# The identity in the chunks' state matrices: sixteen TensorE products per group, or an addend of VectorE

## The chip, the cores and the metric

One NeuronCore of a Trainium2 chip runs the program. The metric is device microseconds (us) of one execution. Engines run their own instruction streams in order and meet only through semaphores: TensorE (PE), VectorE (DVE), ScalarE (ACT), GpSimd (POOL) and SyncE (SP, which here issues the DMAs). TensorE writes to PSUM, and VectorE and ScalarE read it from there.

## The reference, cut to what matters

Two blocks on 512 tokens of width 1024 in f32. The second has a time mixing with one recurrence per token and head (8 heads of 64):

```
state = state * w_t + sa[..., None] * (kk_t * a_t) + v_t[..., None] * k_t
y_t   = einsum('bhvk,bhk->bhv', state, r_t)          # sa = state @ (-kk_t)
```

The kernel does this in chunks of 64 tokens. Over a chunk the state goes through a matrix of the form "decay times (identity plus a product)" and gets an addend. The identity of that sum is what this case is about.

## The kernel before, in words

The second block covers the last 280 us or so of the program. Its input projection and output projection are products of 128x128 weights with 128x512 activations, each as three f32r products (lines 621 to 623: high with high, high with low, low with high). A tile of weights is split by ScalarE (L1293, `whi`) and VectorE (L1845, `wlo`).

The heads are taken in four groups f = 0 to 3 of two heads (128 channels). For each group there are two generators on every engine: `prep(f)` (token shift, decay, keys; beside the projection tiles of window f) and `rwkv(f)` (the chunk algebra; beside the tiles of window f + 1, for f = 3 beside the output projection). `step()` takes one piece of `rwkv` and then one piece of `prep`. It runs on TensorE after every three projection products, and on the other engines at the same count, so the `yield`s of each engine say at which projection step a piece is queued. All order is written out by hand in this way, and no engine overtakes itself.

In `rwkv(f)` the part around the change runs as follows.

- VectorE (L2471) and ScalarE (L1737) copy the solved matrices `QG` out of PSUM.
- TensorE forms, for 8 chunks of 2 heads, the 16 transposed 64x64 matrices `QG` with `Bn` (L1134) and adds to each the identity, as a product of `I64` with itself (L1137), in banks 3 and 4. `s_p` then counts 3f + 1. Then come the chunks' addends (L1142, L1145) in banks 5 and 6, and `s_p` counts 3f + 2. Two heads and two chunk parities take the four 64x64 quarters of the array in turn.
- ScalarE copies the 16 matrices into `Pb` (L1744, two instructions of 64 partitions, one for each head) and counts `s_pv`. `Pb` is block diagonal, and its zeros were written once by GpSimd.
- VectorE scales the addends into `CS` (L2476) and counts `s_pe`.
- The chain over chunks c = 1 to 6: TensorE multiplies `Pb` of c by the state `CS` of c (L1158), VectorE scales and adds (L2486) and gives the next state. The first L1158 waits for `s_pv` and `s_pe`, the others for the L2486 before them. Between them TensorE does the products of L1162, L1168 and L1173 and three projection products for each step.

VectorE runs `prep(f + 1)` in between: L2364 to L2385 (keys), L2314 and L2316 (token shift), L2392 and L2395.

Of the kernel before, what the change touches and what calls it, by code (L numbers as in the profile page):

```python
# [9 lines left out]
ALU = mybir.AluOpType  # L10
ACTF = mybir.ActivationFunctionType
# [22 lines left out]
def build_program(nc, A, out, blocks):  # L34
# [91 lines left out]
    Z = {n[0]: t for n, t in zip(names2, region(0, *names2))}  # L126
# [8 lines left out]
    BK = [PS[:, i, :] for i in range(8)]  # L135
# [133 lines left out]
    s_q, s_qa, s_qd, s_p, s_pv, s_pe = (sem(n) for n in ("s_q", "s_q_act", "s_q_dve", "s_p", "s_p_act", "s_p_dve"))  # L269
# [18 lines left out]
    for q in range(32):  # L288
        g, j = divmod(q, 4)
# [97 lines left out]
    pair = lambda b: PS[:, b:b + 2, 0:256].rearrange("p a (b t) -> p a b t", b=4)  # L387
# [207 lines left out]
    def pe_program(pe):  # L595
# [83 lines left out]
        for c in range(NC):  # L679
            ms = pe.matmul(BK[7][:, c * 128:(c + 1) * 128], small[:, 4 + c:5 + c].to_broadcast([P, P]), ident[:, :],  # L680
                           start=True, stop=True)
# [171 lines left out]
        for j in range(8):  # L853
            half, jj = divmod(j, 4)
            t = tile0[("v", j)]
# [3 lines left out]
            for c in range(NC):  # L859
# [4 lines left out]
                for kk in range(2):  # L864
# [3 lines left out]
                    ms = pe.matmul(h4(bank[:, :]), Hh[:, k, tok], wlo[s][:, at, :], start=False, stop=k == KT - 1)  # L868
# [161 lines left out]
        HALF = [slice(0, 64), slice(64, 128)]  # L1030
        QUADS = [(par, h) for par in range(2) for h in range(2)]

        def rwkv(f):
            KR, bt, kt = Z[f"KR{f % 2}"], Z[f"bt{f % 2}"], Z[f"kt{f % 2}"]
            Vn, Bn, Kn, KA, QG = (Z[n] for n in ("Vn", "Bn", "Kn", "KA", "QG"))
            Ln, Xx, Tt, AU, RB, RK, Ww = (Z[n] for n in ("Ln", "Xx", "Tt", "AU", "RB", "RK", "Ww"))
            Pb, Sb, CS, Rp, I64, YT = (Z[n] for n in ("Pb", "Sb", "CS", "Rp", "id64", "YT"))
            nat = lambda t, par, h, j: t[HALF[par], j * 128 + h * 64:j * 128 + h * 64 + 64]
# [24 lines left out]
            for j in range(4):  # L1063
                for par, h in QUADS:
                    c = 2 * j + par
                    ms = pe.matmul(BK[5 + h][HALF[par], j * 64:(j + 1) * 64], KR[HALF[h], 0, c * 64:(c + 1) * 64],
                                   bt[HALF[h], c * 64:(c + 1) * 64], start=True, stop=True)
# [12 lines left out]
            for j in range(4):  # L1080
                for par in range(2):
                    for h in range(2):
                        ms = pe.matmul(BK[5 + par][HALF[par], j * 128 + h * 64:j * 128 + h * 64 + 64],
                                       mat(AU, par, h, j), nat(Vn, par, h, j), start=True, stop=True)
# [4 lines left out]
            for q in range(1, 6):  # L1089
# [4 lines left out]
                for j in range(4):  # L1094
                    for par, h in QUADS:
                        ms = pe.matmul(BK[3 + par][HALF[h], j * 64:(j + 1) * 64], mat(Ln, par, h, j), mat(Xx, par, h, j),  # L1096
                                       start=True, stop=True)
# [4 lines left out]
                for j in range(4):  # L1102
                    for par, h in QUADS:
                        ms = pe.matmul(BK[5 + par][HALF[h], j * 64:(j + 1) * 64], mat(Xx, par, h, j), I64[HALF[par], :],  # L1104
                                       start=True, stop=True)
# [4 lines left out]
                for j in range(4):  # L1110
                    for par, h in QUADS:
                        ms = pe.matmul(BK[3 + h][HALF[par], j * 64:(j + 1) * 64], matT(Tt, par, h, j), matT(Ww, par, h, j),  # L1112
                                       start=True, stop=True)
# [7 lines left out]
            for j in range(4):  # L1121
                for par, h in QUADS:
                    ms = pe.matmul(BK[3 + 2 * par + h][HALF[par], j * 128:(j + 1) * 128], mat(Xx, par, h, j),
                                   KA[HALF[par], j, h, :, :], start=True, stop=True)
# [6 lines left out]
            pe.wait_ge(s_nat, 4 * f + 4)  # L1131
            for j in range(4):
                for par, h in QUADS:
                    pe.matmul(BK[3 + par][HALF[h], j * 64:(j + 1) * 64], QG[HALF[par], h, j, 0, :], nat(Bn, par, h, j),  # L1134
                              start=True, stop=False)
                for par, h in QUADS:
                    ms = pe.matmul(BK[3 + par][HALF[h], j * 64:(j + 1) * 64], I64[HALF[par], :], I64[HALF[par], :],  # L1137
                                   start=False, stop=True)
            ms.then_inc(s_p, 1)
            for j in range(4):  # L1140
                for par, h in QUADS:
                    pe.matmul(BK[5 + par][HALF[h], j * 64:(j + 1) * 64], nat(Kn, par, h, j), nat(Vn, par, h, j),  # L1142
                              start=True, stop=False)
                for par, h in QUADS:
                    ms = pe.matmul(BK[5 + par][HALF[h], j * 64:(j + 1) * 64], nat(Bn, par, h, j), QG[HALF[par], h, j, 1, :],  # L1145
                                   start=False, stop=True)
# [5 lines left out]
            for c in range(1, 7):  # L1152
# [6 lines left out]
                if c == 1:  # L1159
                    for j in range(4):  # L1160
                        for par, h in QUADS:
                            ms = pe.matmul(BK[3 + par][HALF[h], j * 64:(j + 1) * 64], QG[HALF[par], h, j, 0, :],  # L1162
                                           mat(RB, par, h, j), start=True, stop=True)
                    ms.then_inc(s_p, 1)
                if c == 2:
                    for j in range(4):
                        for par, h in QUADS:
                            pe.matmul(BK[5 + par][HALF[h], j * 64:(j + 1) * 64], nat(Vn, par, h, j), mat(RK, par, h, j),  # L1168
                                      start=j == 0, stop=False, skip_group_check=True)
# [9 lines left out]
            for c in range(1, 8):  # L1179
                j, par = divmod(c, 2)  # L1180
# [42 lines left out]
        t = tile0[("o7", 6)]  # L1223
# [9 lines left out]
        t = tile0[("o8", 0)]  # L1233
# [39 lines left out]
    def act_program(act):  # L1273
# [430 lines left out]
        def rwkv(f):  # L1704
            KA, QG, Pb, Sb, CS = (Z[n] for n in ("KA", "QG", "Pb", "Sb", "CS"))
            for i in range(REST if f == 0 else 0):
                yield
            act.wait_ge(s_q, f)
            act.activation(c8(Z["Xx"][:, :]), Z["id64"][:, :].unsqueeze(1).to_broadcast([P, 8, 64]),
                           ACTF.Copy).then_inc(s_id, 1)  # L1710
            natural(f, 0, Z["Vn"][:, :])
            for i in range(3):
                yield
            for i in range(2):
                yield
            act.wait_ge(s_gr, 4 * f + 4)
            act.activation(KA[0:64, :, :, 1, :], BK[5][0:64, :].rearrange("p (j h v) -> p j h v", j=4, h=2),
                           ACTF.Copy).then_inc(s_avc, 1)
            act.wait_ge(s_nt, 4 * f + 2)
            act.activation(KA[:, :, :, 0, :], BK[7][:, :].rearrange("p (j h k) -> p j h k", j=4, h=2),  # L1720
                           ACTF.Copy).then_inc(s_nat, 1)
            yield
            for q in range(1, 6):
                n = 5 * f + q
                act.wait_ge(s_lw, 2 * n - 1)
                act.activation(Z["Ww"][:, :].rearrange("p (a t) -> p a t", a=2), PS[:, 3:5, 0:256],
                               ACTF.Copy).then_inc(s_ww, 1)
                act.wait_ge(s_lw, 2 * n)
                act.activation(Z["Tt"][:, :].rearrange("p (a t) -> p a t", a=2), PS[:, 5:7, 0:256],
                               ACTF.Copy).then_inc(s_ww, 1)  # L1730
                yield
                yield
                if q <= 2:
                    natural(f, 1 + q, Z[("Bn", "Kn")[q - 1]][:, :])
                yield
            act.wait_ge(s_q, f + 1)
            act.activation(QG[0:64, :, :, :, :].rearrange("p h j a t -> p h (j a t)"), PS[0:64, 3:5, :],  # L1737
                           ACTF.Copy).then_inc(s_qa, 1)
            yield
            yield  # L1740
            act.wait_ge(s_p, 3 * f + 1)
            for h in range(2):
                hs = slice(64 * h, 64 * h + 64)
                e = act.activation(Pb[hs, :, hs].rearrange("p (j a) t -> p a j t", a=2), pair(3)[hs, :, :, :], ACTF.Copy)  # L1744
            e.then_inc(s_pv, 1)
            yield
            yield
            if f in (1, 2):
                yield
            for c in range(1, 7):  # L1750
                if c == 4:
                    act.wait_ge(s_sc, 6 * f + 3)
                    for h in range(2):
                        hs = slice(64 * h, 64 * h + 64)
                        e = act.activation(Sb[hs, 1:5, hs], CS[hs, 1:5, :], ACTF.Copy)
                    e.then_inc(s_sb, 1)
                yield
            act.wait_ge(s_sc, 6 * f + 6)
            for h in range(2):
                hs = slice(64 * h, 64 * h + 64)  # L1760
                e = act.activation(Sb[hs, 5:8, hs], CS[hs, 5:8, :], ACTF.Copy)
            e.then_inc(s_sb, 1)
            yield
            act.wait_ge(s_y, f + 1)
            act.wait_ge(s_gn, f)
            if f == 0:
                act.wait_ge(s_x2, 9)
            act.activation(Z["YT"][:, :].rearrange("p (j a t) -> p a j t", j=4, a=2), pair(5), ACTF.Copy).then_inc(s_yc, 1)
            yield
            act.wait_ge(s_gmd, f + 1)  # L1770
            act.activation(Z["GQ"][:, :], Z["YT"][:, :], ACTF.Square).then_inc(s_gs, 1)
            yield
            yield
            for i in range((4, 7, 0, 0)[f]):
                yield
            act.wait_ge(s_gm, 2 * f + 2)
            act.activation(Z["GQ"][:, :], BK[7][:, :], ACTF.Sqrt, bias=GEPS, scale=1.0 / 64).then_inc(s_gs, 1)
            yield
            yield
# [39 lines left out]
    def dve_program(v):  # L1819
# [312 lines left out]
        for c in range(NC):  # L2132
            e = v.tensor_scalar(V[:, c, :], V[:, c, :], small[:, 16 + c:17 + c], None, ALU.mult)
# [297 lines left out]
        def rwkv(f):  # L2431
# [39 lines left out]
            v.tensor_copy(QG[64:128, :, :, :, :].rearrange("p h j a t -> p h (j a t)"), PS[64:128, 5:7, :]).then_inc(s_qd, 1)  # L2471
            yield
            yield
            v.wait_ge(s_p, 3 * f + 2)
            v.wait_ge(s_ip, f + 1)
            v.tensor_tensor(CS[:, 1:9, :].rearrange("p (j a) t -> p a j t", a=2), pair(5),  # L2476
# [178 lines left out]
```

## Time and profile before

| | |
|---|---|
| median of 3 runs | 1449.18 us (1447.69 to 1449.83) |
| the profiled execution, its own time | 1447.83 us |
| its span, first to last instruction | 1446.6 us |
| mean granted TensorE clock | 0.996 of 2.4 GHz |
| busy: TensorE, VectorE, ScalarE | 99%, 61%, 43% of the span |

The time outside the span is 1447.83 − 1446.6 = 1.2 us. Busy shares are averages over the whole program. What a change in one stage is worth is read from the order in which the engines reach their waits there, so most of the rows below are instructions in order of time. f32 products of lines 1134 to 1173 are seen in the trace as two passes each, so the 64 identity products of the program are 128 rows.

### The profile page before, as it was taken

Reading aid. Unit: us, or ns where it says so; the run is one execution under the profiler, and the core shown is the slowest. Engines: PE = TensorE matmul, PEld = TensorE weight load, DVE = VectorE, ACT = ScalarE, POOL = GpSimd, SP = SyncE. Lnnn points to the kernel's source line nnn. Section 1 sums busy time; section 2 is a strip of 40 time slices with the busy share of each in tenths; the row PEclk is TensorE's granted clock in tenths of the full one; section 3 lists DMA queues with packets and bytes.
Section 4 is the critical chain, followed back from the end, with each engine's and each line's share of the span. In section 5 each row is a group of like instructions: output and inputs, shape, how many; then the busy total and the mean of one; then the engine's idle time right before and its main releaser. Section 6 shows DMA issues by size and latency. Waiting matters only on the chain.

```text
span 1446.6 us, 25206 instructions
## 1 busy us (share of the span) xinstructions
PE 1426.7 (99%) x9965; PEld 1141.6 (79%) x9965; DVE 882.3 (61%) x1251; ACT 625.6 (43%) x976; POOL 195.9 (14%) x228
## 2 busy tenths in 40 slices
PE   8999999999999999999999999999999999999898
PEld 5788888887888887888878888888888777777677
DVE  4777777777545756855556432344345876666736
ACT  4665655555554323232334322244233454453535
POOL 0000000000048888800006000000000000000000
PEclk9999999999999999999999999999999999999999
DMA  9454443444355665533323333333332311211111
GB/s 336 122 148 117 135 114 110 138 125 123 104 157 167 174 173 156 168 98 88 102 73 103 98 101 93 91 98 102 102 88 73 88 47 46 59 45 43 44 51 59
DMA packets 266188, 157.69 MB, mean 109 GB/s; under 512 B 5797, under 2 KB 254938, under 8 KB 266074
## 3 DMA queue, kind: packets, MB, share of 16 engines
q1 hardware_dynamic: 266074, 156.07, 37.0%
q8 instruction: 83, 1.36, 0.4%
q14 instruction: 31, 0.25, 0.1%
HBM read 153.82 MB, written 2.23 MB: 108 GB/s over the span
## 4 chain that ended last, share of the span: by engine, by line
PE 92%; DVE 4%; ACT 2%; issue 1%; POOL 0%; DVEq 0%; ACTq 0%; POOLq 0%
PE PS L621 24%; PE PS L622 23%; PE PS L623 23%; PE PS L796 1%; PE PS L866 1%; PE PS L822 1%; PE PS L868 1%; PE PS L867 1%; PE PS L1096 1%; PE PS L1112 1%; DVE Hl L1857 1%; PE PS L654 1%; PE PS L801 1%; PE PS L813 1%; PE PS L1104 1%
## 5 line engine op out<-in xcount | busy, mean ns | idle before, releaser
L621 PE MATMUL PS<-Hh,whi 128*128 128x512 f32 x1162 | 477.5, 411 | 2.8 <-DVE Hl L1857 2.3
L623 PE MATMUL PS<-Hh,wlo 128*128 128x512 f32 x1162 | 453.6, 390 | 0.0
L622 PE MATMUL PS<-Hl,whi 128*128 128x512 f32 x1162 | 453.5, 390 | 0.0
L1845 DVE TENSOR_TENSOR wlo<-raw,whi 128x1024 fp32r<-128x1024 f32 (+1 forms) x211 | 280.5, 1330 | 111.8 <-ACT whi L1293 111.0
L1293 ACT ACTIVATE whi<-raw 128x1024 fp32r<-128x1024 f32 (+1 forms) x211 | 221.2, 1048 | 167.9 <-PE PS L623 145.6
L621 PEld LDWEIGHTS PS<-Hh,whi 128*128 128x128 f32 x1162 | 218.3, 188 | 64.7 <-issue 18.6
L623 PEld LDWEIGHTS PS<-Hh,wlo 128*128 128x128 f32 x1162 | 218.2, 188 | 46.6
L622 PEld LDWEIGHTS PS<-Hl,whi 128*128 128x128 f32 x1162 | 218.6, 188 | 44.9 <-issue 4.8
L519 POOL TENSOR_TENSOR mbuf<-mbuf,cact 128x1024 f32<-128x1024 f32 x32 | 63.0, 1968 | 414.8 <-DMA mbuf<-in_w_mod_dram 414.8
L621 PE MATMUL PS<-YBh,whi 128*128 128x512 f32 x256 | 99.6, 389 | 0.0
L622 PE MATMUL PS<-YBl,whi 128*128 128x512 f32 x256 | 99.6, 389 | 0.0
L623 PE MATMUL PS<-YBh,wlo 128*128 128x512 f32 x256 | 99.6, 389 | 0.0
L524 POOL TENSOR_TENSOR mbuf<-mbuf 128x512 f32<-128x512 f32 x64 | 90.6, 1416 | 5.0
L1986 DVE SCALAR_TENSOR_TENSOR tmp<-xr,pcA,tmp 128x512 f32<-128x512 f32 x96 | 71.7, 747 | 6.9 <-ACT tmp L1381 5.4
L2267 DVE TENSOR_TENSOR tmp<-tmp 128x512 f32<-128x512 f32 x32 | 22.2, 693 | 56.1 <-ACT tmp L1581 56.1
L623 PEld LDWEIGHTS PS<-YBh,wlo 128*128 128x128 f32 x256 | 48.0, 188 | 10.1
L621 PEld LDWEIGHTS PS<-YBh,whi 128*128 128x128 f32 x256 | 48.0, 188 | 10.0
L622 PEld LDWEIGHTS PS<-YBl,whi 128*128 128x128 f32 x256 | 48.0, 188 | 9.9
L1581 ACT ACTIVATE tmp<-PS 128x512 f32<-128x512 f32 x32 | 19.1, 597 | 74.9 <-PE PS L623 73.5
L621 PE MATMUL PS<-R2h,whi 128*128 128x512 f32 x128 | 50.2, 392 | 0.0
L622 PE MATMUL PS<-R2l,whi 128*128 128x512 f32 x128 | 49.8, 389 | 0.0
L623 PE MATMUL PS<-R2h,wlo 128*128 128x512 f32 x128 | 49.8, 389 | 0.0
(411 smaller groups left out, 1879.4 us busy)
## 6 DMA issues: line engine op xcount, KB each, us to landing
raw<-in_w_in_dram SPq DMA_DIRECT2D x106, 512.0 KB, 3.9
raw<-in_w_ff_dram SPq DMA_DIRECT2D x64, 512.0 KB, 3.6
mbuf<-in_w_mod_dram SPq DMA_DIRECT2D x32, 512.0 KB, 3.7
wm<-in_w_mod_dram SPq DMA_DIRECT2D x8, 1024.0 KB, 9.6
crow<-cum_rows SPq DMA_DIRECT2D x32, 256.0 KB, 4.5
raw<-in_w_branch_ssm_dram SPq DMA_DIRECT2D x16, 512.0 KB, 3.4
erow<-exp_rows SPq DMA_DIRECT2D x24, 256.0 KB, 5.0
raw<-in_w_out_dram SPq DMA_DIRECT2D x10, 512.0 KB, 3.4
```

What stands on the lines that cost most here:

```text
L519: pool.tensor_tensor(w[:, :, :], w[:, :, :], cact[:, :].unsqueeze(2).to_broadcast([P, KT, P]), ALU.mult).then_inc(s_pool, 1)
L524: pool.tensor_tensor(w[:, 0:n, :], w[:, 0:n, :], w[:, n:2 * n, :], ALU.add).then_inc(s_pool, 1)
L621: pe.matmul(bank[:, :], whi[s][:, k, :], xh[:, kk, :], start=kk == 0, stop=False)
L622: pe.matmul(bank[:, :], whi[s][:, k, :], xl[:, kk, :], start=False, stop=False)
L623: last = pe.matmul(bank[:, :], wlo[s][:, k, :], xh[:, kk, :], start=False, stop=t == end - 1 and k == (order or range(kt))[-1])
L654: pe.matmul(h4(BK[bank][:, :]), identb[:, :], identb[:, :].unsqueeze(1).to_broadcast([P, 4, P]), start=True, stop=True)
L796: ms = pe.matmul(to(a), xdt[n % 2][:, h * 64:(h + 1) * 64], dec[n % 2][:, h * 128:(h + 1) * 128], start=True, stop=c == 0)
L1293: act.activation(whi[s][:, 0:kt, :], raw[s][:, 0:kt, :], ACTF.Copy).then_inc(s_whi, 1)
L1581: act.activation(q[:, :], bank[:, :], ACTF.Relu).then_inc(s_relu, 1)
L1845: v.tensor_tensor(wlo[s][:, 0:kt, :], raw[s][:, 0:kt, :], whi[s][:, 0:kt, :].bitcast(F32), ALU.subtract).then_inc(s_wlo, 1)
L1986: e = v.scalar_tensor_tensor(out=a[:, :], in0=b[:, tap:tap + T], scalar=cw(tap, tile), in1=a[:, :], op0=ALU.mult, op1=ALU.add)
L2267: v.tensor_tensor(q[:, :], q[:, :], q[:, :], ALU.mult).then_inc(s_f2, 1)
```

## The change: what it does, and the diff

TensorE no longer multiplies the identity with itself. VectorE takes over the two copies into `Pb` from ScalarE and adds the identity on the way, `id64` being read again for each of the 8 matrices of an instruction. It does so in `rwkv`, after the copy of `QG` and ahead of the scaling into `CS`. The semaphores stay as they were: the adds wait for `s_p` at 3f + 1 and count `s_pv`.

```diff
@@ pe rwkv
             for j in range(4):
                 for par, h in QUADS:
-                    pe.matmul(BK[3 + par][HALF[h], j * 64:(j + 1) * 64], QG[HALF[par], h, j, 0, :], nat(Bn, par, h, j),
-                              start=True, stop=False)
-                for par, h in QUADS:
-                    ms = pe.matmul(BK[3 + par][HALF[h], j * 64:(j + 1) * 64], I64[HALF[par], :], I64[HALF[par], :],
-                                   start=False, stop=True)
+                    ms = pe.matmul(BK[3 + par][HALF[h], j * 64:(j + 1) * 64], QG[HALF[par], h, j, 0, :],
+                                   nat(Bn, par, h, j), start=True, stop=True)
             ms.then_inc(s_p, 1)
@@ act rwkv
             yield
             yield
-            act.wait_ge(s_p, 3 * f + 1)
-            for h in range(2):
-                hs = slice(64 * h, 64 * h + 64)
-                e = act.activation(Pb[hs, :, hs].rearrange("p (j a) t -> p a j t", a=2), pair(3)[hs, :, :, :], ACTF.Copy)
-            e.then_inc(s_pv, 1)
             yield
             yield
@@ dve rwkv
             yield
             yield
+            v.wait_ge(s_p, 3 * f + 1)
+            for h in range(2):
+                hs = slice(64 * h, 64 * h + 64)
+                e = v.tensor_tensor(Z["Pb"][hs, :, hs].rearrange("p (j a) t -> p a j t", a=2), pair(3)[hs, :, :, :],
+                                    Z["id64"][hs, :].unsqueeze(1).unsqueeze(1).to_broadcast([64, 2, 4, 64]), ALU.add)
+            e.then_inc(s_pv, 1)
             v.wait_ge(s_p, 3 * f + 2)
```

VectorE in group 0, kernel before: from the last weight split (`wlo`) to the chain's second step; `wk`, `kt`, `tmp`, `rb` belong to `prep(1)`.

```order
L1845 TENSOR_TENSOR wlo2<-raw2,whi2 128x1024 [waits s_tile,s_whi]
L2382 TENSOR_TENSOR wk4<-wk4,tmp1 128x512 [waits s_dve_own]
L2476 TENSOR_TENSOR CS<-PS,fx0 128x2x4x64 [waits s_fx,s_p]
L2385 TENSOR_TENSOR kt1<-wk4,wk3 128x512 [waits s_dve_own]
L2314 TENSOR_TENSOR tmp0<-pad1 128x512 [waits s_shift,s_pad]
L2316 SCALAR_TENSOR_TENSOR rb<-tmp0,pcC,pad1 128x512 [waits s_dve_own]
L2486 SCALAR_TENSOR_TENSOR CS<-PS,fx0,CS 128x64 [waits s_p_dve,s_s] x2
```

The same place in the changed kernel (its lines from L1134 on have lower numbers: L2474 is L2476 of before, L2484 is L2486).

```order
L1837 TENSOR_TENSOR wlo2<-raw2,whi2 128x1024 [waits s_tile,s_whi]
L2374 TENSOR_TENSOR wk4<-wk4,tmp1 128x512 [waits s_dve_own]
L2469 TENSOR_TENSOR Pb<-PS,id64 64x2x4x64 [waits s_p]
L2469 TENSOR_TENSOR Pb<-PS,id64 64x2x4x64
L2474 TENSOR_TENSOR CS<-PS,fx0 128x2x4x64 [waits s_fx,s_p]
L2377 TENSOR_TENSOR kt1<-wk4,wk3 128x512 [waits s_dve_own]
L2306 TENSOR_TENSOR tmp0<-pad1 128x512 [waits s_shift,s_pad]
L2308 SCALAR_TENSOR_TENSOR rb<-tmp0,pcC,pad1 128x512 [waits s_dve_own]
L2484 SCALAR_TENSOR_TENSOR CS<-PS,fx0,CS 128x64 [waits s_p_dve,s_s] x2
```

Two instructions stand between the keys' product and the scaling into `CS`. Everything behind them on VectorE keeps its order, and the first step of the chain over chunks is the fourth instruction behind the scaling.

VectorE in groups 1 and 2, changed kernel (shown of group 1); before, the rows are the same without the two of L2469.

```order
L2463 COPY QG<-PS 64x1024 [waits s_q]
L2356 SCALAR_TENSOR_TENSOR KR0<-acc,wk0 128x512 [waits s_decay_exp]
L2361 SCALAR_TENSOR_TENSOR acc<-wk1,acc 128x512 [waits s_dve_own,s_sigm]
L2469 TENSOR_TENSOR Pb<-PS,id64 64x2x4x64 [waits s_p]
L2469 TENSOR_TENSOR Pb<-PS,id64 64x2x4x64
L2474 TENSOR_TENSOR CS<-PS,fx1 128x2x4x64 [waits s_fx,s_p]
L2365 TENSOR_TENSOR acc<-acc,tmp1 128x512 [waits s_dve_own]
```

Here the two adds come directly behind L2361, the L2369 of before, and ahead of the same scaling.

## Rows read from the trace of the kernel before

**Rows 1.** The page: busy time of the engines with share of the span

```profile
PE 1426.7 (99%) x9965; PEld 1141.6 (79%) x9965; DVE 882.3 (61%) x1251; ACT 625.6 (43%) x976; POOL 195.9 (14%) x228
```

**Rows 2.** The page: chain that ended last, by engine

```profile
PE 92%; DVE 4%; ACT 2%; issue 1%; POOL 0%; DVEq 0%; ACTq 0%; POOLq 0%
```

**Rows 3.** Groups by shape, 1180 to 1410 us: count | busy us, mean ns | idle, releaser

```profile
L1744 ACT ACTIVATE Pb<-PS 64x512 f32<-64x512 f32 x8 | 4.7, 591 | 5.9 <-PE PS L1137 5.8
...
L1137 PE MATMUL PS<-id 64*64 64x64 f32 x128 | 4.0, 218 | 0.0
...
L2476 DVE TENSOR_TENSOR CS<-PS,fx 128x512 f32<-128x512 f32 x4 | 2.8, 692 | 3.5 <-PE PS L1145 3.5
```

**Rows 4.** Waits, 1180 to 1410 us: us in total, times, longest

```profile
DVE CS L2476 <- PE PS L1145: 3.5, 3, 1.7
...
PEld PS L1158 <- DVE CS L2486: 1.4, 3, 0.5
...
PE PS L1005 <- DVE acc L2556: 2.8, 1, 2.8
```

**Rows 5.** Timeline, group 0, TensorE: start us, us, engine, line [idle before <-releaser]

```profile
1191.50 0.30 PE L1137 MATMUL PS<-id 64*64 64x64 f32 x8
...
1192.32 0.30 PE L1142 MATMUL PS<-Vn,Kn 64*64 64x64 f32 x8
...
1194.63 0.41 PEld L1158 LDWEIGHTS PS<-CS,Pb 128*128 128x128 f32 x2
...
1196.63 0.30 PEld L1158 LDWEIGHTS PS<-CS,Pb 128*128 128x128 f32 x2 [0.37 <-DVE CS L2486]
```

**Rows 6.** Timeline, group 0, VectorE

```profile
1192.99 0.68 DVE L2382 TENSOR_TENSOR wk<-wk,tmp 128x512 f32<-128x512 f32 x1
1193.71 0.69 DVE L2476 TENSOR_TENSOR CS<-PS,fx 128x512 f32<-128x512 f32 x1
1194.32 0.68 DVE L2385 TENSOR_TENSOR kt<-wk 128x512 f32<-128x512 f32 x1
...
1196.30 0.28 DVE L2486 SCALAR_TENSOR_TENSOR CS<-PS,fx,CS 128x64 f32<-128x64 f32 x1
1197.11 0.28 DVE L2486 SCALAR_TENSOR_TENSOR CS<-PS,fx,CS 128x64 f32<-128x64 f32 x1 [0.53 <-PE PS L1158]
```

**Rows 7.** Timeline, group 1, all engines

```profile
1256.30 0.69 DVE L2369 SCALAR_TENSOR_TENSOR acc<-wk,acc 128x512 f32<-128x512 f32 x1
...
1257.87 0.69 DVE L2476 TENSOR_TENSOR CS<-PS,fx 128x512 f32<-128x512 f32 x1 [0.88 <-PE PS L1145]
...
1259.92 0.55 DVE L2379 TENSOR_SCALAR tmp<-wk,kah,omka 128x512 f32<-128x512 f32 x1
...
1260.38 1.22 DVE L1845 TENSOR_TENSOR wlo<-raw,whi 128x1024 fp32r<-128x1024 f32 x1
...
1261.52 0.28 DVE L2486 SCALAR_TENSOR_TENSOR CS<-PS,fx,CS 128x64 f32<-128x64 f32 x1
...
1261.85 0.30 PEld L1158 LDWEIGHTS PS<-CS,Pb 128*128 128x128 f32 x2 [0.53 <-DVE CS L2486]
```

**Rows 8.** Timeline, group 3, all engines

```profile
1398.15 0.30 PE L1137 MATMUL PS<-id 64*64 64x64 f32 x8
...
1398.51 1.19 ACT L1744 ACTIVATE Pb<-PS 64x512 f32<-64x512 f32 x2 [1.69 <-PE PS L1137]
...
1399.44 0.69 DVE L2476 TENSOR_TENSOR CS<-PS,fx 128x512 f32<-128x512 f32 x1 [1.69 <-PE PS L1145]
...
1400.80 0.33 PE L1158 MATMUL PS<-CS,Pb 128*128 128x64 f32 x2
```

**Rows 9.** Windows: us, busy of each engine, then PEclk, DMA share, GB/s

```profile
360.00:362.00 2.00, 0.50 (x3) 0.40 (x3) 0.69 (x1) 1.87 (x4) 0.00 (x0) 1.00 0.95 292
362.00:364.00 2.00, 2.00 (x12) 1.61 (x11) 0.00 (x0) 0.25 (x1) 0.00 (x0) 1.00 0.85 188
...
1364.00:1365.00 1.00, 1.00 (x10) 0.35 (x12) 1.00 (x3) 0.00 (x0) 0.00 (x0) 0.50 0.00 0
```

## The prediction, made before the changed kernel was run

> **What bounds the kernel now.** I read the page first, then the grouped instructions and the waits of the stretch in which the changed lines run, and last the timeline around each of the four groups. TensorE is busy 99% of the span and VectorE 61% [rows 1], and the chain that ended last lies to 92% on TensorE [rows 2]. By these averages alone, work taken from TensorE is time won, and VectorE has room. The waits say that this does not hold at the place of the change. TensorE stood three times at the chain over chunks, at a L1158 that waited for VectorE's L2486, 1.4 us in all [rows 4]. In group 0 this was the second L1158, at 1196.63 us after 0.37 us of idleness [rows 5]. In group 1 it was again the second, at 1261.85 us after 0.53 us [rows 7]. The third, in group 2, is the same pattern. So in groups 0 to 2 VectorE sets the time of this point, and only in group 3 does TensorE. The reason is VectorE's queue: it runs without idle time from L2382 at 1192.99 us to L2486 at 1196.30 us, since the chain's first step is queued behind three instructions of the next group's preparation [rows 6].
>
> **What goes from TensorE.** The 64 products with the identity are 128 passes [rows 3]. Their mean of 218 ns is not their price, because four quarters of the array overlap. The price is the step between starts: from the run of L1137 at 1191.50 us to the run of L1142 at 1192.32 us there are seven runs of 8 passes (L1137 and L1134 in turn) [rows 5], so 8 passes take 0.82 / 7 = 0.117 us, 14.6 ns each. A group has 32 such passes, 0.47 us, and the four groups 1.87 us. That is the most the change could give.
>
> The Trainium skill has a floor for this: "TensorE: Matmul & The Clock Gate", section "Back-to-back issue gap", lets no matmul of up to 64 columns start less than about 25 ns behind another. By it a group's passes would be worth 0.80 us instead of 0.47, and the sum below would be 0.33 us lower, since only group 3 keeps this gain. The trace speaks against it, with 14.6 ns for passes in different quarters.
>
> **What goes from ScalarE.** Eight copies of 0.591 us [rows 3] go. ScalarE had been idle 1.69 us before them in group 3 [rows 8], and what stood behind them are copies and weight splits whose takers on VectorE are queued behind other VectorE work: in group 1 the next `wlo` starts only at 1260.38 us, directly behind L2379 [rows 7]. Worth nothing, and the cover is VectorE's own queue. Were that cover gone, nothing would be lost either, because this edit only frees.
>
> **What comes to VectorE.** Two adds per group, each of 64 partitions and 512 elements, PSUM and `id64` in, `Pb` out. The trace has no such instruction. The nearest is L2476: two operands, one of them broadcast, the other from the same kind of PSUM pair, 512 elements, 0.692 us long [rows 3]. But the next instruction starts 0.61 us after it (1193.71 to 1194.32 us) [rows 6], so what it costs the queue is p = 0.61 us. Upper bound: the step from L2382 to L2476, 0.72 us. Lower bound: the step from L2379 to L1845, 0.46 us (1259.92 to 1260.38) [rows 7], an instruction with one tensor operand. I take 0.61.
>
> A page speaks against moving such a copy: "Advanced Engine Details and Errata", section "The Read-Write Bubble", of the Trainium skill says that VectorE exposes the memories' latency between two instructions, and that ScalarE lies nearer to PSUM. The trace agrees in part: 0.692 us on VectorE against 0.591 us on ScalarE, while successive instructions overlap by 0.08 us. With the whole 0.69 us for p the sum would be +1.8 us.
>
> **Group 0.** The queue has no gap, so the adds push L2476, L2385, L2314, L2316 and the first L2486 by 2p = 1.22 us. The first L1158 waits for L2476, which ended at 1194.40 and would end at 1195.62 us. TensorE would come there at 1194.63 − 0.47 = 1194.16 us and stand for some 1.4 us. The second L1158 waits for the first L2486, 1196.30 + 1.22 = 1197.52 us instead of 1196.30, so it starts 1.22 us later than 1196.63. The second L2486 then waits for TensorE again, as before (0.53 us [rows 6]), and from there on both engines carry the same delay. TensorE's 0.47 us lies inside this wait and is lost. Group 0: +1.22 us.
>
> **Groups 1 and 2.** Here VectorE had been idle 0.88 us before L2476 (of the 3.5 us in three waits [rows 4]: 0.88, 0.88, 1.69). L1134 is through 0.47 us sooner, so `s_p` is there when L2369 leaves the queue free, at 1256.30 + 0.61 = 1256.91 us. L2476 then starts at 1256.91 + 1.22 = 1258.13 instead of 1257.87 us: +0.26 us. From there to L2486 at 1261.52 us there is no gap [rows 7], so the second L1158 comes 0.26 us later, and TensorE's 0.47 us again only lengthens its wait. In general 2p − 0.96 for each. Groups 1 and 2: +0.52 us.
>
> **Group 3.** The output projection gives VectorE little to do. The last L1137 began at 1398.15 us and ScalarE took up its result at 1398.51 us, 0.36 us later [rows 8]. In the changed kernel the result is there 0.47 us sooner, at 1398.04 us; the adds take 1.22 us, and L2476 runs from 1399.26 to 1399.95 us (its own operand is there at 1399.44 − 0.47 = 1398.97 us). TensorE reaches the first L1158 at 1400.80 − 0.47 = 1400.33 us, with its weight load some 0.2 us ahead of that. The wait is met with 0.2 us to spare, and the 0.47 us is won: −0.47 us. It is lost from 2p of about 1.4 us on.
>
> **Sum.** 1.22 + 0.52 − 0.47 = +1.27 us, in general 6p − 2.39 us: +0.4 us for p = 0.46 and +1.9 us for p = 0.72. Nothing later gives the delay back, since the waits behind these points are for results that follow from them. This is against the profiled execution's 1447.83 us (span 1446.6 and 1.2 around it), which gives 1449.1 us. That execution lies 1.35 us under the median of the runs, 1449.18 us, and the changed kernel is measured by a median too, so I forecast 1449.18 + 1.27, rounded 1450.5 us.
>
> **Rivals.**
>
> 1. TensorE's saving is the time: −1.87 us, 1447.3 us. For it speak the 99% and the 92% [rows 1, 2]. It needs VectorE's delay to be absorbed, and VectorE had no idle time between L2382 and L2486 [rows 6]. Partly true (some of group 0's delay absorbed later) it gives about 1449 us, no change.
> 2. The adds are dear, and the kernel is slower by more than 0.2%. The place is VectorE's queue ahead of L2476, in all four groups. If the broadcast and the strided `Pb` doubled the work, p would be near the 1.14 us step of a 1024 element instruction (L1845 at 1260.38 to L2486 at 1261.52 [rows 7]): 6 × 1.14 − 2.39 = +4.45 us, and group 3 pays another 2.28 − 1.4 = 0.9 us, together 1454.5 us. It decides from p = 0.88 us on (+2.9 us). Against it: L2476 has the same shape and a broadcast, and ScalarE's copy into the same strides took 0.591 us.
> 3. The clock. TensorE's new stand of about 1.4 us in group 0 could take it to the lower level. After its longest stand in this stretch, 2.8 us ahead of L1005 [rows 4], the granted clock was 0.50 at 1364 us, the 1.2 GHz level, while after 1.5 us idle within 360 to 362 us it stayed at 1.00, 2.4 GHz [rows 9]. If it fell for 4 us (I assume this length), work of 2 us would take 4: +2 us on top, 1452.5 us. The nearer row says that it holds.
>
> **How the numbers follow.** About 0.2%, 2.9 us, is what a measurement of this kernel can tell from no change. The forecast (its own range 1449.5 to 1451.5 us) has a chance of 0.66, rival 1 in full or in part 0.16, rival 2 0.10, rival 3 0.08. The forecast lies within 0.2% altogether, and so does nearly all of rival 1; half of rival 3 and all of rival 2 do not. With medians that differ by some tenths from one measurement to the next this makes faster 0.04, same 0.81, slower 0.15. The range of 8 in 10 takes the bounds of p, +0.4 and +1.9 us, and the runs' own spread of 2.1 us: 1448.4 to 1452.5 us.
>
> **What would show it.** Right: the adds at 0.6 to 0.7 us each, back to back; a wait of TensorE of over 1 us at the first L1158 of group 0 with L2476's counterpart as its releaser; the wait at the second L1158 of groups 1 and 2 grown from 0.53 to about 1.3 us; no new wait in group 3, and there the distance from the first L1134 to the first L1158 shorter by 0.47 us. Wrong: an add over 0.85 us; no growth of TensorE's waits in groups 0 to 2 although the products are gone; a granted clock under 1.00 between 1195 and 1202 us.

## The result, and the profile after

| | median us | runs | range |
|---|---|---|---|
| before | 1449.13 | 20 | 1447.10 to 1451.36 |
| after | 1452.12 | 20 | 1448.88 to 1455.76 |

The ratio is 1.0019, with a 95% interval of 1.0012 to 1.0026: slower by 1.7 to 3.8 us. The ratio lies just inside the 0.2% that the prediction had called no change, the upper end of its interval outside. Later the changed kernel was measured again, under the label e10_again: 1450.78 us against 1448.98, ratio 1.0012 (1.0003 to 1.0021). A small loss is sure. Its size is easier to read from the trace.

The profiled execution of after took 1453.63 us, 5.80 more than that of before. Most of this has nothing to do with the change. The first L1134 of group 0, ahead of which no changed instruction runs, already began 3.66 us later (1191.33 and 1194.99 us), because the clock was low twice more on the way there than before. The windows show it: time, busy of each engine, granted clock, DMA share, GB/s. First after, then before.

```profile
14.00:18.00 4.00, 3.88 (x24) 1.98 (x28) 3.63 (x7) 0.00 (x0) 0.00 (x0) 0.62 1.11 370
574.00:578.00 4.00, 3.25 (x9) 2.26 (x8) 4.00 (x6) 0.63 (x1) 1.51 (x2) 0.59 0.00 0
```

```profile
14.00:18.00 4.00, 4.00 (x42) 1.61 (x40) 2.31 (x4) 0.38 (x1) 0.00 (x0) 1.00 1.11 371
574.00:578.00 4.00, 4.00 (x19) 3.33 (x20) 4.00 (x8) 2.21 (x3) 1.59 (x2) 1.00 0.19 56
```

So I compare distances in which this cancels as long as the clock within them is alike: from the first weight load of L1134 in a group to that in the next, and from the last to the end of the span. The timelines of before at groups 0, 1 and 3, then of after:

```profile
1191.33 0.21 PEld L1134 LDWEIGHTS PS<-Bn,QG 64*64 64x64 f32 x8 [0.37 <-issue]
...
1255.71 0.21 PEld L1134 LDWEIGHTS PS<-Bn,QG 64*64 64x64 f32 x8 [0.36 <-issue]
...
1397.28 0.21 PEld L1134 LDWEIGHTS PS<-Bn,QG 64*64 64x64 f32 x8 [0.36 <-issue]
```

```profile
1194.99 0.56 PEld L1134 LDWEIGHTS PS<-Bn,QG 64*64 64x64 f32 x32 [0.37 <-issue]
...
1260.81 0.56 PEld L1134 LDWEIGHTS PS<-Bn,QG 64*64 64x64 f32 x32 [0.37 <-issue]
...
1403.55 0.56 PEld L1134 LDWEIGHTS PS<-Bn,QG 64*64 64x64 f32 x32 [0.36 <-issue]
```

Group 0 takes 65.82 us instead of 64.38 (+1.44), group 1 67.63 instead of 67.03 (+0.60), group 2 75.11 instead of 74.54 (+0.57; it begins at 1322.74 us before and at 1328.44 after). From there the end comes after 48.75 instead of 49.32 us (−0.57). That last stretch holds much work behind the chain, so for group 3 I also use the distance to the load of `GQ`'s product (L1191, after: L1188): 16.95 and 16.56 us, −0.39. The whole is +2.04 us by the span. In the second execution of after (e10_again) the four are +1.42, +0.61, +0.58 and −0.40, by the span +1.86. Inside group 2 the clock was low once in before (at 1364 us) and once in after (at 1370 us), and not at all in e10_again; the distance of e10_again is nevertheless after's to 0.01 us.

The page after, engines' busy time, in answer to [rows 1]:

```profile
PE 1428.6 (98%) x9837; PEld 1141.8 (79%) x9837; DVE 889.0 (61%) x1259; ACT 621.2 (43%) x968; POOL 195.6 (13%) x228
```

128 matmul rows (64 products of two passes) and 8 copies fewer, 8 adds more, and the shares hardly move. What moved are the waits, 1180 to 1412 us, in answer to [rows 4] (us in total, times, longest):

```profile
PE PS L1155 <- DVE CS L2484: 2.4, 3, 1.1
...
PEld PS L1155 <- DVE CS L2484: 3.7, 3, 1.6
PE PS L1155 <- DVE CS L2474: 1.4, 1, 1.4
```

L1155 is the chain's product (L1158 before), L2474 and L2484 are VectorE's L2476 and L2486. The three waits of the weight loads grew from 1.4 to 3.7 us, and one more of 1.4 us came at the start of group 0's chain. Group 0 after, VectorE and TensorE, in answer to [rows 5, 6]:

```profile
1196.65 0.69 DVE L2374 TENSOR_TENSOR wk<-wk,tmp 128x512 f32<-128x512 f32 x1
1197.37 1.39 DVE L2469 TENSOR_TENSOR Pb<-PS,id 64x512 f32<-64x512 f32 x2
1198.79 0.69 DVE L2474 TENSOR_TENSOR CS<-PS,fx 128x512 f32<-128x512 f32 x1
1199.40 0.68 DVE L2377 TENSOR_TENSOR kt<-wk 128x512 f32<-128x512 f32 x1
...
1199.63 0.41 PE L1155 MATMUL PS<-CS,Pb 128*128 128x64 f32 x2 [1.42 <-DVE CS L2474]
...
1201.72 0.30 PEld L1155 LDWEIGHTS PS<-CS,Pb 128*128 128x128 f32 x2 [0.60 <-DVE CS L2484]
```

The two adds hold the queue from 1197.37 to 1198.79 us, 0.71 us each, and TensorE stands 1.42 us at the chain's first product. Group 1, in answer to [rows 7]:

```profile
1261.39 0.69 DVE L2361 SCALAR_TENSOR_TENSOR acc<-wk,acc 128x512 f32<-128x512 f32 x1
1262.11 1.39 DVE L2469 TENSOR_TENSOR Pb<-PS,id 64x512 f32<-64x512 f32 x2
1263.54 0.69 DVE L2474 TENSOR_TENSOR CS<-PS,fx 128x512 f32<-128x512 f32 x1
...
1267.52 0.30 PEld L1155 LDWEIGHTS PS<-CS,Pb 128*128 128x128 f32 x2 [1.55 <-DVE CS L2484]
```

VectorE now has no gap here, and the wait at the second L1155 grew from 0.53 to 1.55 us. Group 3, in answer to [rows 8]:

```profile
1404.32 1.39 DVE L2469 TENSOR_TENSOR Pb<-PS,id 64x512 f32<-64x512 f32 x2 [0.29 <-PE PS L1134]
1405.74 0.69 DVE L2474 TENSOR_TENSOR CS<-PS,fx 128x512 f32<-128x512 f32 x1
1406.55 0.30 PEld L1155 LDWEIGHTS PS<-CS,Pb 128*128 128x128 f32 x2 [0.21 <-issue]
```

TensorE comes with almost no wait: this is the one group in which its time was won. From the first L1134 to the first chain product it takes 3.05 us (1403.56 to 1406.61), 0.47 us less than before, as in e1 below; the 0.21 us of idle time ahead of the weight load is new, and some 0.05 us of the gain is gone at the next load. The clock behind group 0's new stand stayed at its upper level, 1.00 (2.4 GHz), in answer to [rows 9]:

```profile
1201.00:1203.00 2.00, 1.84 (x38) 1.27 (x37) 1.47 (x5) 0.00 (x0) 0.00 (x0) 1.00 0.00 0
```

### The profile page after: what moved, and what is told of

The parts are those of the page before. It is cut to its first block, busy times and chain, and to the rows that moved or that the text cites. A ratio compares the mean times of both kernels' runs of the same rounds, so it can differ in the third digit from the quotient of the medians.

```text
span 1452.3 us, 24950 instructions
## 1 busy us (share of the span) xinstructions
PE 1428.6 (98%) x9837; PEld 1141.8 (79%) x9837; DVE 889.0 (61%) x1259; ACT 621.2 (43%) x968; POOL 195.6 (13%) x228
## 4 chain that ended last, share of the span: by engine, by line
PE 92%; DVE 5%; ACT 2%; issue 1%; POOL 0%; DVEq 0%; POOLq 0%; ACTq 0%
PE PS L621 24%; PE PS L622 23%; PE PS L623 23%; PE PS L796 1%; PE PS L866 1%; PE PS L822 1%; PE PS L867 1%; PE PS L868 1%; PE PS L1096 1%; PE PS L654 1%; PE PS L1112 1%; DVE Hl L1849 1%; PE PS L801 1%; PE PS L813 1%; PE PS L1104 1%
```

## The experiments

Each was read by the distances above. The table gives them as differences from before (g3 is the distance to `GQ`'s product). The ratio is that of the times, with its 95% interval.

| | g0 | g1 | g2 | g3 | ratio |
|---|---|---|---|---|---|
| after | +1.44 | +0.60 | +0.57 | −0.39 | 1.0019 (1.0012 to 1.0026) |
| e10_again | +1.42 | +0.61 | +0.58 | −0.40 | 1.0012 (1.0003 to 1.0021) |
| e1_products_gone | −0.03 | −0.46 | −0.48 | −0.46 | 0.9984 (0.9975 to 0.9993) |
| e2_add_beside | +1.38 | +0.61 | +0.56 | +0.05 | 1.0013 (1.0004 to 1.0022) |
| e3b_full_identity | +1.42 | +0.61 | +0.59 | −0.40 | one time, 1452.28 us |
| e4b_adds_twice | +4.29 | +4.89 | +4.83 | +0.98 | 1.0080 (1.0062 to 1.0097) |
| e5_split | −0.01 | −0.01 | +0.02 | −0.38 | 0.9997 (0.9988 to 1.0006) |
| e6_one_step_later | +0.74 | +0.58 | +0.58 | −0.40 | 1.0014 (1.0003 to 1.0024) |
| e7_split_later | −0.23 | 0.00 | +0.01 | −0.38 | 0.9996 (0.9987 to 1.0006) |
| e8_one_add | +0.95 | +0.11 | +0.21 | +0.07 | 1.0004 (0.9995 to 1.0012) |
| e9_compact | +0.40 | +0.37 | +0.43 | +0.55 | 1.0007 (0.9998 to 1.0016) |

**The halves of the change.** e1 is the kernel before with TensorE's edit alone:

```diff
-                for par, h in QUADS:
-                    ms = pe.matmul(BK[3 + par][HALF[h], j * 64:(j + 1) * 64], I64[HALF[par], :], I64[HALF[par], :], ...)
```

> Only TensorE's part of the change: the 16 identity products of a group are gone, ScalarE still copies Pb, VectorE adds nothing, so the identity is left out of the chunks' matrices. Measure: the distance from a group's first L1134 to the next group's (for group 3 to the end of the span), 64.38, 67.03, 74.54 and 49.3 us before. Theory A (VectorE's queue sets the time in groups 0 to 2, TensorE in group 3): group 0 unchanged (0.0), because the first L2486 stands behind VectorE's own queue; groups 1 and 2 shorter by 0.47 us each, because there VectorE had been idle before L2476 and starts it 0.47 us sooner; group 3 shorter by 0.47; together -1.4 us. Theory B (TensorE's saving counts everywhere and the loss comes from elsewhere, as from the clock): -0.47 us in each group, -1.9 us.

The removal saves 0.46 to 0.48 us in three groups and nothing in group 0, where the weight load of TensorE's second chain product stood 0.60 us instead of 0.37:

```profile
1195.92 0.30 PEld L1155 LDWEIGHTS PS<-CS,Pb 128*128 128x128 f32 x2 [0.60 <-DVE CS L2483]
```

In groups 1 and 2 the saving is real without the adds, since VectorE's 0.88 us of idleness there [rows 7] shrinks with it. There it was TensorE that VectorE waited for.

e2 is the changed kernel with the identity's products put back (the diff of e1 reversed); the identity is then counted twice.

> Only VectorE's and ScalarE's part: the identity products stay on TensorE, and VectorE's two adds replace ScalarE's copies, so the identity is counted twice. Theory A: group 0 +1.43 us (two adds of 0.71 us in a queue without a gap), groups 1 and 2 +0.58 each (the adds start when L2369 leaves the queue free, whether the products are there or not), group 3 about +0.1 (the adds end a little after TensorE arrives), together +2.7 us. Theory B: no change, 0 us.

With the products there, groups 0 to 2 are as slow as without them, and only group 3 changes, by 0.44 us. So the two halves don't add up: in the changed kernel TensorE's saving is worth 0.4 us, where e1 has 1.43. The rest is shut into VectorE's waits.

**Why an add costs 0.71 us and not 0.61.** e3b is the changed kernel; it lets the adds read an ordinary tile that holds the identity eight times, in place of the repeated operand:

```diff
+                    own(v.tensor_copy(c8(tmp[2][:, :]), Z["id64"][:, :].unsqueeze(1).to_broadcast([P, 8, 64])))
...
-                                    Z["id64"][hs, :].unsqueeze(1).unsqueeze(1).to_broadcast([64, 2, 4, 64]), ALU.add)
+                                    two(tmp[2][hs, :]), ALU.add)
```

> The changed kernel, but the adds take the identity from a tile that holds it eight times (filled once, before group 0) instead of reading one 64x64 block again for each matrix. Theory A1 (the 0.71 us instead of 0.61 us from start to start belong to instructions with a repeated operand): each add starts 0.61 us after its predecessor, L2474's counterpart still 0.72 us after the second add; the distance from a group's first L1134 to the next one's is 1.2 us longer than before in group 0 and 0.35 in groups 1 and 2. Theory A2 (they belong to the half of the partitions, the strided output, or PSUM): 0.71 us, and the distances of the changed kernel, +1.44, +0.60 and +0.57 us.

```profile
1195.54 0.68 DVE L2374 TENSOR_TENSOR wk<-wk,tmp 128x512 f32<-128x512 f32 x1
1196.26 1.39 DVE L2471 TENSOR_TENSOR Pb<-PS,tmp 64x512 f32<-64x512 f32 x2
1197.68 0.69 DVE L2476 TENSOR_TENSOR CS<-PS,fx 128x512 f32<-128x512 f32 x1
```

Still 1.42 us for two, so the repeated operand is not the reason. e8 makes the two one add of 128 partitions, with `Pb` kept without its zero blocks and a chain step of two 64x64 products:

```diff
-                pe.matmul(BK[7][:, 0:64], Pb[:, c, :], CS[:, c, :], start=True, stop=True).then_inc(s_s, 1)
+                for h in range(2):
+                    ms = pe.matmul(BK[7][HALF[h], 0:64], Pb[HALF[h], c, 0:64], CS[HALF[h], c, :], start=True, stop=True)
+                ms.then_inc(s_s, 1)
...
+            v.tensor_tensor(Z["Pb"][:, :, 0:64].rearrange("p (j a) t -> p a j t", a=2), pair(3),
```

> The changed kernel with a compact Pb (128 partitions x 8 chunks x 64, the zeros left out): one add of 128 partitions fills it, and a step of the chain over chunks is two 64x64 products in two quarters of the array in place of one 128x128. Theory A: VectorE carries one add instead of two: 0.71 us if each instruction costs that whatever its partitions (A2a), 0.61 if half partitions were what cost the 0.10 us (A2b). The first chain product then comes 0.7 us sooner than in the changed kernel in group 0, and against before group 0 +0.7 us, groups 1 and 2 -0.1 to 0, group 3 -0.4, apart from what the chain's products in quarters cost or save, which no row of before shows; that part is read from the run beside it. Theory B (the queue of VectorE is not what counts): the first chain product of group 0 as late as in the changed kernel.

```profile
1194.80 0.68 DVE L2376 TENSOR_TENSOR wk<-wk,tmp 128x512 f32<-128x512 f32 x1
1195.52 0.69 DVE L2469 TENSOR_TENSOR Pb<-PS,id 128x512 f32<-128x512 f32 x1
1196.13 0.68 DVE L2474 TENSOR_TENSOR CS<-PS,fx 128x512 f32<-128x512 f32 x1
```

The one add on all partitions is followed after 0.61 us, an add on 64 after 0.71, though both last 0.69 us. The strided output isn't the reason either: the two adds that e4b (below) puts into scratch, with no gaps between the matrices, take 1.40 us.

But half the partitions can't be the whole reason. The 128-partition add of e8 itself starts 0.72 us behind L2376 (1194.80 to 1195.52 us), without overlap, and so does L2476 in the kernel before, 0.72 us behind L2382 [rows 6]. These steps share something else with those of the 64-partition adds: the first partition changes. The copy of `QG`, VectorE's last read of PSUM ahead of them, begins at partition 64 and the instruction at 0; in the changed kernel the adds begin at 0 and at 64, and the scaling at 0 again. In e8 the add and the scaling both begin at 0, and they overlap. No run has two instructions on 64 partitions with the same first partition behind one another, so that the change of the first partition is the reason, and not the width, fits all these rows but was not tested by itself.

e8 also changes the chain, so e9 has this by itself: the kernel before with e8's chain products and one copy of ScalarE for the two.

> The kernel before with the same compact Pb: the identity products stay, ScalarE copies Pb in one instruction of 128 partitions, and the chain's steps are two 64x64 products. It shows what the chain in quarters costs or saves by itself. Theory A: no change up to the first chain product (ScalarE's copy was not waited for). From there on between -0.2 and +0.2 us per step, 24 steps: -4.8 to +4.8 us; I take 0, since a change of the array's form is made before each step now instead of behind it.

A chain in quarters is dearer, 0.37 to 0.55 us per group of six steps, 1.75 us in all, 0.07 us a step on average. The steps differ. In group 0 the third one, which other products in quarters follow, takes 1.05 us from the projection product ahead of it to the one behind (before: 1.12); the fourth, between projection products alone, takes 0.59 us (before: 0.37). Ahead of such a step TensorE has an issue gap, which in the kernel before stands nowhere ahead of the chain's last four products of this group:

```profile
1200.13 0.14 PEld L1159 LDWEIGHTS PS<-CS,Pb 64*64 64x64 f32 x2 [0.37 <-issue]
...
1201.76 0.19 PEld L1159 LDWEIGHTS PS<-CS,Pb 64*64 64x64 f32 x4 [0.36 <-issue]
```

Against e9 the single add is worth +0.55, −0.26, −0.22 and −0.48 us. The prediction's forms with one add of 0.61 give +0.61, −0.35, −0.35 and −0.47; the 0.72 us ahead of the add accounts for the 0.1 us or so that groups 1 and 2 lack.

**How the loss grows.** e4b puts two further adds, into scratch, ahead of the two:

```diff
+                v.tensor_tensor(two(tmp[2][hs, :]), pair(3)[hs, :, :, :],
+                                Z["id64"][hs, :].unsqueeze(1).unsqueeze(1).to_broadcast([64, 2, 4, 64]), ALU.add)
```

> The changed kernel with VectorE's adds doubled: ahead of the two adds into Pb stand two of the same shape into a scratch tile. Theory A (VectorE's queue sets the time): another 2 x 0.71 = 1.43 us in each of groups 0, 1 and 2, so distances from L1134 to L1134 of 67.2, 69.1 and 76.5 us, and in group 3, from the first L1134 to the load of GQ's product, 18.0 us instead of 16.56; against the kernel before +7.8 us. Theory B (the adds are hidden, the loss is elsewhere): the distances of the changed kernel, 65.8, 67.6, 75.1 and 16.6 us.

The weight load of the first chain product moved by what was expected, 1.40, 1.41 and 1.40 us in groups 0 to 2, and group 3 grew over after by 1.37 us. But groups 0 to 2 grew by 2.85, 4.29 and 4.26 us. The windows of e4b show where the rest lies:

```profile
1196.00:1198.00 2.00, 0.00 (x0) 0.00 (x0) 1.94 (x4) 0.00 (x0) 0.00 (x0) 1.00 0.70 208
1200.00:1202.00 2.00, 1.83 (x37) 1.33 (x35) 1.44 (x5) 0.00 (x0) 0.00 (x0) 0.68 0.00 0
1202.00:1204.00 2.00, 2.00 (x13) 1.59 (x16) 0.52 (x2) 0.00 (x0) 0.00 (x0) 0.50 0.03 8
1270.00:1272.00 2.00, 2.00 (x35) 1.69 (x32) 1.31 (x3) 0.00 (x0) 0.00 (x0) 0.50 0.85 235
```

```profile
1265.96 0.41 PE L1155 MATMUL PS<-CS,Pb 128*128 128x64 f32 x2 [1.08 <-DVE CS L2478]
1269.11 0.69 PE L1155 MATMUL PS<-CS,Pb 128*128 128x64 f32 x2 [1.22 <-DVE CS L2488]
```

In group 0 TensorE stood 2.83 us until 1198.36; the granted clock fell behind this and was 0.50, the 1.2 GHz level, at 1202 us. An estimate from the windows: 2 us at 0.68 and 2 us at 0.50 are 1.6 us of full speed, about the 1.45 us that group 0 grew beyond the adds. In group 1 (and in group 2 alike) the clock fell, 0.75 in the window from 1268 to 1270 us and 0.50 after it, behind two stands of 1.08 and 1.22 us, each shorter than the changed kernel's 1.42 in its group 0. So the prediction's third rival exists. The changed kernel's one stand of 1.42 us didn't set it off in either profile, but a longer one did, and so did two shorter ones that followed one another.

**Where VectorE has room.** e5 is the kernel before with the change made only where the waits allowed it: in group 3 for both halves, in groups 1 and 2 for one, in group 0 not at all.

```diff
+    ADDED = {0: (), 1: (1,), 2: (1,), 3: (0, 1)}
...
+                                   nat(Bn, par, h, j), start=True, stop=h in ADDED[f])
...
+                    if h not in ADDED[f]:
+                        ms = pe.matmul(BK[3 + par][HALF[h], j * 64:(j + 1) * 64], I64[HALF[par], :], I64[HALF[par], :],
```

> The change put only where VectorE has room: group 0 as before, groups 1 and 2 half (head 1 by VectorE's add, head 0 by 8 identity products and ScalarE's copy), group 3 wholly. Theory A: group 0 unchanged; groups 1 and 2 shorter by 0.23 us each (one add of 0.72 fits into the 0.88 us that VectorE had been idle, and 8 of 16 products are gone); group 3 shorter by 0.39 as in the changed kernel; together -0.85 us against before, ratio 0.9994. Theory B (every add costs its length): groups 1 and 2 longer by 0.5 us each, together +0.6 us.

Half of the products gone was worth nothing, against 0.23 us expected. The distances of the four groups add up to −0.38 us, all of it from group 3. Group 1 of e5, TensorE:

```profile
1258.10 0.29 PE L1136 MATMUL PS<-Bn,QG 64*64 64x64 f32 x6
...
1258.34 0.29 PE L1136 MATMUL PS<-Bn,QG 64*64 64x64 f32 x6
...
1258.57 0.29 PE L1136 MATMUL PS<-Bn,QG 64*64 64x64 f32 x6
```

A step over j has 12 passes instead of 16 and still takes 0.235 us. The remaining identity products of one `h` lie in two of the four quarters, where they follow one another as before; the freed quarters merely stand empty.

**Moving the chain.** e6 is the changed kernel with one more piece of the projection ahead of group 0's chain (ScalarE gives one yield back at its end):

```diff
-            if f in (1, 2):
+            if f in (0, 1, 2):
...
-            for i in range((4, 7, 0, 0)[f]):
+            for i in range((3, 7, 0, 0)[f]):
```

> The changed kernel, and in group 0 the chain over chunks begins one projection step (three products of 0.23 us on TensorE) later on all engines, so that TensorE has work while VectorE adds; VectorE's order up to the first L2484 is the same. Theory A: group 0 wins 0.70 us of its 1.44 us back, L1134 to L1134 65.1 us; the other groups as in the changed kernel; together +1.3 us against before. Theory C (the stand itself is not the loss, but what follows on VectorE after the adds is): group 0 stays at 65.8 us.

```profile
1197.43 0.41 PE L1155 MATMUL PS<-CS,Pb 128*128 128x64 f32 x2 [0.74 <-DVE CS L2474]
```

Three projection matmuls of 0.23 us fill 0.70 us of the stand, and group 0's loss falls from 1.44 to 0.74 us. e7 joins this with e5:

> The split of the run before it (group 0 as in the kernel before, groups 1 and 2 half, group 3 wholly) and in group 0 the chain one projection step later. Theory A: group 0 wins the 0.37 us that TensorE stood at the second L1158 before; groups 1 and 2 0.23 each, group 3 0.39: together -1.2 us against before, ratio 0.9992.

In group 0 it gained 0.23 us, one such matmul. The four distances add up to −0.60 us (by the span from group 0 on −0.94), and the ratio of the times is 0.9996 (0.9987 to 1.0006): no version is shown to beat the kernel before by its time except e1, which leaves the identity out.

**The clock as a hidden cost.** e10_again is the changed kernel unchanged.

> The changed kernel once more, for a second profile and more times. Theory A: the distances of its first profile again, +1.44, +0.60, +0.57 us and in group 3 -0.39 us up to the load of GQ's product, in the time +2 us against before. Theory D (TensorE's stand of 1.4 us in group 0 lets the clock fall in some executions, and that is the rest of the 3.0 us between the medians): a granted clock of 0.5 behind the stand, or a mean clock of the runs lower than that of before.

The distances came again within 0.02 us, and the clock behind the stand was 1.00 again. The mean granted clock of after's 20 runs was 0.9965 and of e10_again's runs 0.9976. The kernel before, measured beside the later runs, had 0.9956 to 0.9964: the change brings no loss of clock that these show.

## Why the prediction came out as it did

- **The number.** The median, 1452.12 us, lies in the range of 8 in 10 (1448.4 to 1452.5), 0.4 us under its upper end, and outside the forecast's own 1449.5 to 1451.5. The +1.27 us lies under the first measurement's interval (1.7 to 3.8 us) and within the second's (0.4 to 3.0). That the first median still fell into the range is in part luck: the mechanism accounts for 2.0 to 2.2 of its 3.0 us.
- **What bounds this place.** Right in group 0; for groups 1 and 2 "VectorE sets the time" was said too broadly, since e1 saves 0.46 and 0.48 us there, but the form 2p − 0.96 has VectorE's wait in it. e1 shows TensorE's 0.47 us worthless in group 0, e2 shows it worthless in groups 0 to 2 once the adds stand in VectorE's queue.
- **TensorE's saving.** Right in size: 0.46 to 0.48 us in e1 for 32 passes, as 32 × 14.6 ns says, and not the 0.80 us that the floor in the Trainium skill ("TensorE: Matmul & The Clock Gate", "Back-to-back issue gap") would make it. But "passes times step" holds only where all quarters are relieved together (e5).
- **ScalarE's copies: nothing.** No run took them away alone. e1 keeps them and saves what was computed, and what the changed kernel loses is accounted for by the adds.
- **The adds.** This is the term that was mis-sized. The prediction took p = 0.61 us from L2476 and its successor, both of which begin at partition 0; the adds alternate between the halves and cost 0.71 us. The prediction's upper bound, 0.72, held it. A row of before could have told: VectorE's copy L2471, on partitions 64 to 127, is 1.23 us long, and the next, on all of them, starts 1.27 us after it, without overlap.

```profile
1395.80 1.23 DVE L2471 COPY QG<-PS 64x1024 f32<-64x1024 f32 x1 [2.11 <-PE PS L1123]
1397.07 0.69 DVE L2583 TENSOR_TENSOR XT<-XT,PS 128x512 f32<-128x512 f32 x1
```

- **The groups.** Group 0: predicted +1.22, measured +1.44; 2 × 0.71 = 1.42 explains it. Groups 1 and 2: predicted +0.26, measured +0.60 and +0.57. Of this 2 × 0.71 − 0.96 = 0.46 is p, and 0.11 is that the first add follows L2361 only after 0.72 us (1261.39 to 1262.11), where the prediction had 0.61. That isn't for its 64 partitions: in e8 the 128-partition add follows the same instruction after 0.72 us too (1259.06 to 1259.78). The prediction had this step before it, as L2382 to L2476, and used it only as a bound of p. Group 3: predicted −0.47, measured −0.39; the adds end at 1405.74 us, and TensorE's load at 1406.55 comes 3.00 us behind the first L1134's, where e1 has 2.82.
- **The sum.** The form 6p − 2.39 gives +1.87 us with 0.71; with 0.11 more in each of groups 1 and 2 it is +2.09. The groups add up to +2.2, by the span +2.04. The forecast was +1.27. The stand (predicted about 1.4 us, measured 1.42) and the second wait of group 1 (predicted about 1.3, measured 1.55) were where they were said to be. The mechanism held, then, and the size of two steps of VectorE was off.
- **The rivals.** TensorE's saving as the time is refuted by e1 and e2. Dear adds: p is 0.71, under the 0.88 from which it would decide (0.84, if group 3's own payment from 2p = 1.4 on is counted, which the prediction left out there). The clock: it stayed up behind the one stand of 1.42 us, and fell in e4b behind 2.83 us and behind 1.08 and 1.22 us together.
- **What stays open.** The medians differ by 2.99 us in the first measurement and 1.80 in the second, against 2.0 to 2.2 in the traces. Both intervals hold the traces' value. Why the first lay higher isn't explained: four of its 20 runs, with a mean clock of 0.994, took 1453.6 to 1455.8 us, and none of e10_again's 11 had so low a clock, but the other 16 still have a median of 1451.7. Low stretches of the clock come and go between executions and make 2 us and more (after's first 1195 us, above).

## What to carry to other kernels

Before moving work from a 99% busy engine to a 61% busy one, look at the waits of the place itself: here the busy engine stood waiting for the idle one, and its queue had no gap. A saving on TensorE counts only where it doesn't end in a wait; if it does, bring other work ahead of that wait. Take the price of an instruction from start to next start, from one with the same partitions as its neighbours have in the new place, and compare variants by distances between landmarks of the trace, which here came again within 0.02 us where the times scatter by 2 and more.

## What the hardware showed that I had not expected

VectorE's add of 512 elements lasts 0.69 us on 64 and on 128 partitions. Its successor starts 0.61 us after it where both begin at partition 0, and 0.71 us where adds on the two halves alternate; a 128-partition instruction whose predecessor in reading PSUM began at partition 64 starts without overlap too, after 0.72 us. Four of 16 passes removed from a step over four quarters save nothing if two quarters keep all of theirs. A 128x128 chain step cut into two 64x64 products costs 0.22 us more between 128x128 products, and nothing where other 64x64 products follow. And two stands of TensorE of 1.08 and 1.22 us were followed by the 1.2 GHz level, where one of 1.42 us was not.
